# Causal attention steps on one core: the scores of a head's last two query tiles in one PSUM bank, with one mask

## The reference, cut to what matters

```python
def masked_softmax(s, mask):
    sf = jnp.where(mask, s.astype(jnp.float32), NEG)
    m = jnp.max(sf, axis=-1, keepdims=True)
    e = jnp.where(mask, jnp.exp(sf - m), 0.0)
    p = e / jnp.maximum(jnp.sum(e, axis=-1, keepdims=True), TINY)
    return p.astype(s.dtype)
...
    def win_block(args):
        qb, kb, vb, tq, tk = args
        diff = tq[:, None] - tk[None, :]
        mask = (tk[None, :] >= 0) & (diff >= 0) & (diff < WINDOW)
        s = jnp.einsum('bgrqd,bgkd->bgrqk', qb, kb) * scale
        p = masked_softmax(s, mask)
        return jnp.einsum('bgrqk,bgkd->bgrqd', p, vb)
...
def mla_attention(...):
    def blk(args):
        qb, tq = args
        s = jnp.einsum('bhqd,bhkd->bhqk', qb, k) * scale
        p = masked_softmax(s, tq[:, None] >= pos[None, :])
        return jnp.einsum('bhqk,bhkd->bhqd', p, v)
```

## Time and profile before

| | us |
|---|---|
| median of three executions | 1565.44 |
| lowest and highest | 1565.34, 1565.99 |
| profiled execution | 1565.64 |
| its span, first to last instruction | 1563.8 |
| TensorE busy | 1525.6 (98%) |
| VectorE busy | 894.2 (57%) |
| ScalarE busy | 715.0 (46%) |
| GpSimd busy | 424.9 (27%) |

### The profile page before, as it was taken

The page is one execution under the profiler, slowest core; times in us unless marked ns, Lnnn a source line. Parts: engine busy times, 40 slices in busy tenths (PEclk is TensorE's granted clock), DMA queues, the critical chain, the costliest instruction groups (busy, mean ns, idle before and its releaser), DMA issues.

```text
span 1563.8 us, 23217 instructions
## 1 busy us (share of the span) xinstructions
PE 1525.6 (98%) x7566; PEld 1261.9 (81%) x7566; DVE 894.2 (57%) x1349; ACT 715.0 (46%) x1313; POOL 424.9 (27%) x442
## 2 busy tenths in 40 slices
PE   6999999999999999999999999999999999999996
PEld 5888878787888888888888888778878888888885
DVE  6764755666654444535566656556675535354455
ACT  6753676874432222222366547768634212222232
POOL 0301666775010110101011036757730201010110
PEclk9999999999999999999999999999999999999998
DMA  5333212124323222223223412111352222322223
GB/s 193 107 135 128 82 61 75 42 87 149 118 86 107 95 94 94 95 95 104 98 82 122 169 67 76 55 68 55 98 173 95 95 94 95 105 96 94 94 94 108
DMA packets 43526, 155.55 MB, mean 99 GB/s; under 512 B 5312, under 2 KB 5312, under 8 KB 43424
## 3 DMA queue, kind: packets, MB, share of 16 engines
q1 hardware_dynamic: 37440, 134.23, 25.6%
q0 software_dynamic: 5408, 17.95, 3.4%
q10 hardware_dynamic: 576, 2.10, 0.4%
HBM read 143.78 MB, written 10.49 MB: 99 GB/s over the span
## 4 chain that ended last, share of the span: by engine, by line
PE 85%; issue 5%; DVE 5%; ACT 3%; POOL 1%; DMA 0%; DVEq 0%; ACTq 0%; POOLq 0%
PE G L1351 14%; PE G L1353 14%; PE G L1352 14%; PE O L1352 8%; PE O L1353 8%; PE O L1351 8%; PE O L1618 3%; PE T L1594 3%; PE S L1577 2%; PE T L1351 2%; PE T L1352 1%; PE T L1353 1%; PE O L1426 1%; PE S L1585 1%; DVE F L1302 1%
## 5 line engine op out<-in xcount | busy, mean ns | idle before, releaser
L578 ACT ACTIVATE wsplit<-stage 128x1024 fp32r<-128x1024 f32 x230 | 243.8, 1060 | 610.2 <-PE G L1353 281.4
L905 DVE TENSOR_TENSOR wsplit<-stage,wsplit 128x1024 fp32r<-128x1024 f32 x184 | 266.3, 1447 | 68.6 <-ACT wsplit L578 62.1
L1351 PE MATMUL G<-xg,wsplit 128*128 128x512 f32 x592 | 243.6, 412 | 13.4 <-DVE xg L909 10.8
L571 POOL TENSOR_TENSOR F<-Y 128x512 f32<-128x512 f32 x64 | 68.5, 1070 | 637.3 <-DVE Y L1319 637.3
L1353 PE MATMUL G<-xg,wsplit 128*128 128x512 f32 x592 | 232.0, 392 | 0.0
L1352 PE MATMUL G<-xg,wsplit 128*128 128x512 f32 x592 | 231.1, 390 | 0.0
L1115 DVE TENSOR_REDUCE nmx<-S 128x1 f32<-128x512 f32 x192 | 93.4, 487 | 96.6 <-PE S L1585 94.4
L1351 PEld LDWEIGHTS G<-xg,wsplit 128*128 128x128 f32 x592 | 112.6, 190 | 36.7 <-DVE xg L909 13.7
L736 ACT ACTIVATE F<-S,nmx 128x512 f32<-128x512 f32 x192 | 101.4, 528 | 69.8 <-DVE nmx L1115 68.8
L1353 PEld LDWEIGHTS G<-xg,wsplit 128*128 128x128 f32 x592 | 111.4, 188 | 24.4
L1352 PEld LDWEIGHTS G<-xg,wsplit 128*128 128x128 f32 x592 | 112.0, 189 | 20.0 <-issue 1.0
(11 more groups left out here) (253 smaller groups left out, 3060.5 us busy)
## 6 DMA issues: line engine op xcount, KB each, us to landing
stage<-units SPq DMA_DIRECT2D x230, 512.0 KB, 3.3
stage_n<-units_n SPq DMA_DIRECT2D x22, 512.0 KB, 3.4
gates<-Y POOLq DMA_DIRECT2D x32, 256.0 KB, 2.9
E<-gates POOLq DMA_DIRECT2D x24, 256.0 KB, 3.8
x<-x_in ACTq DMA_DIRECT2D x4, 512.0 KB, 7.1
F<-gates POOLq DMA_DIRECT2D x8, 256.0 KB, 5.2
out<-F SPq DMA_DIRECT2D x6, 256.0 KB, 2.1
rope<-tables POOLq DMA_DIRECT2D x1, 768.0 KB, 6.8
```

The costliest lines, as they stand in the source:

```text
L571: pool.tensor_tensor(F[:, m % 2, :], Y[:, m % 2, :], Y[:, m % 2, :], ALU.mult)\
L578: act.activation(wslot(u)[:, 0, :], staged(u), ACT.Copy).then_inc(s_whin if u in SN else s_whi, 1)
L905: dve.tensor_tensor(wslot(u)[:, 1, :], staged(u), wslot(u)[:, 0, :], ALU.subtract)\
L1351: pe.matmul(dst, a(0), b(0), start=first, stop=False)
```

## The change

The scores are put in three places per head instead of four. `score_tile(j)` counts n = 3 x head + 0, 1, 2, 2 and takes bank n % 2; the 128-wide job has columns 256 to 383 of the bank that holds the 256-wide one. TensorE issues the products of both in the step of the 256-wide job, and one mask matmul of 256 columns (the causal tile twice, a broadcast operand) covers both diagonal blocks, which stand side by side. In the step of the 128-wide job it issues no scores. VectorE takes both maxima one behind the other in the step of the 256-wide job, and the exponential of the 256-wide job waits for both, so that the two engines don't read the bank at once. The scores of a head's first job now wait for the exponential of job i - 3 instead of i - 2.

```diff
+        def score_tile(j):
+
+            qt = JOBS[j][3]
+            n = 3 * (j // QT) + min(j % QT, 2)
+            at = 2 * P if qt == 0 else 0
+            return SB[n % 2][:, at:at + (qt + 1) * P]
...
                 def exps(i):
                     w = (JOBS[i][3] + 1) * P
-                    act.wait_ge(s_max, l * NJ + (i + 1))
-                    act.activation(prob(i, w), SB[i % 2][:, 0:w], ACT.Exp, bias=nmx[:, i % 4:i % 4 + 1],
+                    act.wait_ge(s_max, l * NJ + (i + (2 if JOBS[i][3] == 1 else 1)))
+                    act.activation(prob(i, w), score_tile(i), ACT.Exp, bias=nmx[:, i % 4:i % 4 + 1],
                                    accum_out=sums[:, i % 4:i % 4 + 1]).then_inc(s_exp, 1)
...
                 for i in range(STEPS):
-                    if i < NJ:
+                    if i < NJ and JOBS[i][3] > 0:
                         max_of(i)
+                    if i < NJ and JOBS[i][3] == 1:
+                        max_of(i + 1)
...
                 def scores(i):
                     t, e, br, qt = JOBS[i]
-                    w = (qt + 1) * P
-                    dst = SB[i % 2]
-                    if i >= 2:
+                    if qt == 0:
+                        return
+                    if i % QT == 0 and i > 0:
+                        pe.wait_ge(s_exp, l * NJ + (i - 2))
+                    elif i >= 2:
                         pe.wait_ge(s_exp, l * NJ + (i - 1))
...
+                    products(i, True)
+                    if qt > 1:
+                        pe.matmul(score_tile(i)[:, qt * P:qt * P + P], identb, causal, start=False, stop=True,
+                                  skip_group_check=True).then_inc(s_scores, 1)
                     else:
...
+                        products(i + 1, False)
+                        bank = SB[(3 * (i // QT) + 2) % 2]
+                        pe.matmul(bank[:, P:3 * P], identb, causal.unsqueeze(1).broadcast_to([P, 2, P]), start=False,
+                                  stop=True, skip_group_check=True).then_inc(s_scores, 2)
```

More of the change, by code:

```diff
@@ L1112, in max_of @@
                 def max_of(i):
-                    w = (JOBS[i][3] + 1) * P
                     dve.wait_ge(s_scores, l * NJ + (i + 1))
-                    dve.tensor_reduce(nmx[:, i % 4:i % 4 + 1], SB[i % 2][:, 0:w], AX.X, ALU.max, negate=True)\
+                    dve.tensor_reduce(nmx[:, i % 4:i % 4 + 1], score_tile(i), AX.X, ALU.max, negate=True)\
                         .then_inc(s_max, 1)
@@ L1567, in _, with products @@
                         hidden_T(0)
+                def products(i, opens):
+                    t, e, br, qt = JOBS[i]
+                    w = (qt + 1) * P
+                    dst = score_tile(i)
+                    if i < NSA_NJ:
+                        for c in range(2):
+                            pe.matmul(dst, QS[:, 2 * t + e, qt * P:w], KN[:, br, t // 2, c, 0:w],
+                                      start=opens and c == 0, stop=False, skip_group_check=True)
+                    else:
+                        a, b = lambda c: MQ[:, t % 2, e, c, qt * P:w], lambda c: MK[:, t % 2, e, c, 0:w]
+                        pe.matmul(dst, a(0), b(0), start=opens, stop=False, skip_group_check=True)
+                        pe.matmul(dst, a(0), b(1), start=False, stop=False, skip_group_check=True)
+                        pe.matmul(dst, a(1), b(0), start=False, stop=False, skip_group_check=True)
@@ L1569, in scores @@
                 def scores(i):
                     t, e, br, qt = JOBS[i]
-                    w = (qt + 1) * P
-                    dst = SB[i % 2]
-                    if i >= 2:
-                        pe.wait_ge(s_exp, l * NJ + (i - 1))
[L1575 to L1578, removed]
-                    else:
[L1580 to L1584, removed]
@@ L1585, in scores @@
-                    pe.matmul(dst[:, qt * P:w], identb, causal, start=False, stop=True).then_inc(s_scores, 1)
+                    if qt == 0:
[3 more added lines that the diff above has]
+                    elif i >= 2:
+                        pe.wait_ge(s_exp, l * NJ + (i - 1))
+                    if i >= NSA_NJ and qt == QT - 1:
+                        pe.wait_ge(s_mlo, l * NMLO + (MLO["MQ", t, e] + 1))
+                        emptied(("MK", t, 0))
```

## The result

The prediction of 1564.7 us, no change, did not hold. The changed kernel takes 1569.58 us (median of 13 executions), the kernel before 1565.99 us (median of 13 beside them): ratio 1.0022, 95% interval 1.0014 to 1.0029. That is 3.6 us slower, just over the bound of 0.2%, which the interval holds, and outside the range of 1562.0 to 1567.4. The profiled execution has a span of 1567.7 us, 3.9 over before.

The account below looks back on a forecast made before the run. TensorE, busy 98% of the span, was taken as the bound. Filled heads -2.5, bare heads +1.6 and steps 32 to 39 +0.2 sum to -0.7 us: 1564.7 from a median of 1565.44, range 1562.0 to 1567.4.

Parts of the forecast that it names:

- TensorE's own row: Heads with a projection piece in the 128-wide step: 0.07 us less each, 36 heads, 2.5 us less in all.
- The first 128-wide product behind a 256-wide one: Moved pair in TensorE's row: first product about 0.12 us behind the 256-wide one, next 0.11 later, 0.23 for both.
- The wide mask's place: TensorE's row: the 256-column mask holds its place 0.04 us, as the 128-wide one does; nothing taken for the width.
- rival 1: The mask pays for its columns: 0.02 instead of 0.07 us gained in 36 heads, 1566.5 us; chance 0.12.
- The MLA heads have three products instead of two in both places, and the same difference.: TensorE's row in MLA heads: the same gain per head as in NSA heads, 0.07 us.
- the 384-wide low part's reader: Output products behind VectorE's subtraction in filled heads: 1.0 us of cover, 0.45 left after the delay, costed at nothing.
- can push ScalarE's next copy, of the 256-wide probabilities, whose readers come a whole step later: Filled heads: the 256-wide exponential, 0.48 us late, can delay this copy, whose readers come late enough; no cost added.
- all ten waits: TensorE's waits in the first layer's steps: all placed in six of 24 heads, steps 32 to 39 and 56 to 71.
- Steps 32 to 39: Heads with five TensorE waits: two gains run into late ScalarE and VectorE; loss of 0.1 us a layer, bounds 0.5.
- Bare heads: Steps 56 to 63, without projection pieces: the uncovered delay costs 0.31 and 0.48 us, 0.8 a layer, 1.6 in all.
- The MLA heads 64 to 71: One wait on VectorE's rotation stays, another has a 0.35 us hole for the moved pair; zero, bounds 0.4 either side.
- Rival 3: Second maximum reaches TensorE in filled heads at the 384-wide subtraction, if delayed 1.04 us; 1568.5 us and more; chance 0.09.

Follow-up runs that it names:

- e3: The changed kernel with two masks of 128 columns in the shared bank in place of the one of 256; 1570.73 us, ratio 1.0031 to the kernel before.
- e5: The changed kernel with the second maximum taken a step later, behind the 256-wide job's exponential, which waits for the first maximum alone; 1565.93 us, ratio 1.0000.
- e6: The changed kernel with VectorE's evacuations ahead of everything else in the 256-wide steps from step 12 on; 1568.98 us, ratio 1.0020 to the kernel before.
- e1: The changed kernel with the merge in the 16 NSA heads of a layer alone, the MLA heads as before; 1567.12 us, ratio 1.0002 to the kernel before.
- e2: The changed kernel with the merge in the 8 MLA heads of a layer alone, the NSA heads as before; 1569.06 us, ratio 1.0022 to the kernel before.

## Why the prediction was wrong

- **TensorE's own row: right, under-sized.** Eleven filled NSA heads a layer gave -0.93 and -0.92, forecast -0.77. That hides two errors: ten of them gained about 0.12 us each instead of 0.07, and the one of steps 12 to 15 lost 0.26. The first 128-wide product behind a 256-wide one starts 0.12 later, as forecast, but the second only 0.06 behind the first instead of 0.11 (below). The wide mask's place costs 0.04, as forecast from the earlier trace rows; rival 1 is out by e3. The Trainium skill, "TensorE: Matmul & The Clock Gate", section "Back-to-back issue gap", has a rule for an isolated matmul that would charge an estimated 53 ns for 128 more columns. No such gap shows behind the mask here: its successor starts 0.04 us behind it.
- **The failed step: "The MLA heads have three products instead of two in both places, and the same difference."** TensorE's row is alike, but not the cover. The NSA heads have no projection piece in the 256-wide step, so what VectorE empties behind its low part is wanted later. In the MLA heads the next piece waits for the bank that VectorE empties last in that very step: cover 0.45 us before, 0.65 needed. I had priced the delay for the 384-wide low part's reader only, 1.0 us of cover, and not for the evacuations behind it. Instead of -0.42 a layer came +1.42 and +1.48. Most of it is the second maximum (e5, with it behind the exponential, has +0.22); the rest is the delay by the moved products themselves.
- **"can push ScalarE's next copy, of the 256-wide probabilities, whose readers come a whole step later"**: not enough. VectorE's low part waits for that copy too and holds up the next evacuation (e6, and steps 12 to 15), at 300.90 even TensorE's reader waits for it, and at the end of the attention the chain reaches GpSimd and a weight split with no slack: +0.65 a layer where nothing was in the sum. The trace of before could have told it: not all ten waits of the earlier trace rows lie in the heads of steps 32 to 39 and 56 to 71. Steps 32 to 39 have four, not five, and one, of 0.34 us for a low part, is at 362.34, behind the last head, and TensorE's wait of 0.94 for the weight split at 368.11 is just outside the window.
- **Bare heads: right.** e1, without MLA heads, has +0.71 and +0.69 in steps 56 to 71, forecast +0.8. The sum is right, the shares are not: the first head cost 0.45 instead of 0.31 and the second, with the wait behind it, 0.23 instead of 0.48. The MLA heads 64 to 71, put at 0 with bounds of 0.4, gave -0.40 (e2), all of it in steps 68 to 71: the moved products fill the idle 0.35 us ahead of the output products at 296.43; the wait for the rotation hardly grows (0.35 before, 0.42 in the changed kernel).
- **Steps 32 to 39: wrong in size.** +0.6 a layer (the table's +0.49 has the filled head of steps 40 to 43 in it), forecast +0.1 with bounds of 0.5. It falls in steps 32 to 35 (+0.73), where three waits for low parts and a bank grow or appear. In steps 36 to 39 the wait for an exponential is gone, as forecast, but the weight load of the output products at 236.34 sits idle for 1.00 us instead of 0.40. e5 has +0.19 in the table's stretch.
- **Rival 3 named the right effect at the wrong place.** The second maximum does reach TensorE in filled heads, but through emptied banks in four MLA heads and one NSA head a layer and through the 256-wide low part at step 72, not through the 384-wide low part in all eighteen, whose cover held at 0.46. Its condition, a delay of 1.04 us, was never met; the bank's cover was met at 0.45.

Sum of the differences between forecast and table, a layer: MLA heads 1.84, the end 0.65, steps 32 to 43 0.46, bare and first MLA heads -0.53, row in 11 NSA heads -0.16: 2.26, and 4.5 for two layers, which leads from -0.7 to +3.9 within 0.1. The upper end of the range was added up a little low (1566.5 and twice 0.55 are 1567.6, not 1567.4); the measured time lies outside either.

The Trainium skill, "PSUM — Partial Sum Buffer", section "PSUM bank collisions raise a hardware error", says that ScalarE and VectorE reading the same partitions of one bank at once raises an error; the exponential's wait for both maxima keeps these reads apart. No run here shows such a collision, and a kernel without either wait wasn't tried.

## What to carry to other kernels

When an operation is moved ahead in an engine's queue, list everything behind it in that queue up to the next point of slack, and for each the first reader with its own cover; the nearest reader need not be the tightest. A cover found in one kind of head holds only for heads with the same pieces in the same steps. Look for waits up to the point where the work next meets, here the first matmul behind the attention, and not only inside the steps that the edit touches. And sharing a bank can be had without tying two reductions to one exponential: here the pair in succession cost 4.2 us of attention (e5 against the changed kernel), and with the second one behind the exponential the kernel was as fast as before.

## What the runs showed of the hardware

The first 128-column fp32r product behind a 256-column one starts 0.12 us behind it (0.11 in the rounded starts here), the second only 0.06 behind the first, the third 0.11 behind the second. All 48 heads of the changed kernel show the 0.06 (timeline of TensorE in one of them):

```profile
304.86 0.28 PE L1589 MATMUL S<-area 128*128 128x256 f32 x1
304.97 0.22 PE L1587 MATMUL S<-area 128*128 128x128 f32 x1
305.03 0.28 PE L1588 MATMUL S<-area 128*128 128x128 f32 x1
305.14 0.27 PE L1589 MATMUL S<-area 128*128 128x128 f32 x1
```

The steps of 1 us outside the attention are short stretches at the clock's lower level, 1.2 GHz. They fall in different places in the traces of these kernels. The executions of the kernel before lie between 1565.21 and 1566.94 us beside the changed one, so medians that differ by up to about 1 us say little. Windows of the changed kernel (third figure from the end is the granted clock):

```profile
90.40:91.80 1.40, 1.40 (x5) 1.06 (x4) 0.39 (x1) 1.36 (x3) 0.00 (x0) 0.50 0.00 0
856.50:860.50 4.00, 4.00 (x31) 3.79 (x31) 1.32 (x2) 2.44 (x6) 0.00 (x0) 1.00 0.22 87
```

and of the kernel before:

```profile
90.20:91.60 1.40, 1.40 (x8) 1.15 (x7) 0.00 (x0) 1.38 (x3) 0.00 (x0) 1.00 0.00 0
855.60:859.60 4.00, 4.00 (x16) 3.49 (x16) 1.15 (x2) 3.79 (x7) 0.00 (x0) 0.57 0.00 0
```

What makes the clock fall at the one place or the other stays open.
